# One-hot tables of the first expert layer: three wide vector operations a group in place of seventeen

## The reference

```python
eidx = jnp.take_along_axis(cidx, sel, axis=-1)
g = jax.nn.softmax(best, axis=-1)
act = jax.nn.gelu(jnp.einsum('td,thkd->thk', xb, u[eidx]).astype(jnp.float32))
return jnp.einsum('thk,thkd->td', (g * act).astype(v.dtype), v[eidx]).astype(h.dtype)
```

## Time and profile before

| | |
|---|---|
| median of 3 executions | 3064.28 us (3061.97 to 3066.18) |
| profiled execution | 3058.98 us, span 3057.2 us |
| the table, first DVE operation of a group to the last copy to `stage` | 799.24 to 893.86 us of the span |
| the stream's first multiply by gates | 923.97 us |
| DVE busy over the span | 2123.6 us, 69% |
| PE busy over the span | 2457.7 us, 80% |

### The profile page before, as it was taken

The page is one execution under the profiler, slowest core; times in us unless marked ns, Lnnn a source line. Parts: engine busy times, 40 slices in busy tenths (PEclk is TensorE's granted clock), DMA queues, the critical chain, the costliest instruction groups (busy, mean ns, idle before and its releaser), DMA issues. The chain is left out here.

```text
span 3057.2 us, 37030 instructions
## 1 busy us (share of the span) xinstructions
PE 2457.7 (80%) x13126; PEld 1869.5 (61%) x13126; DVE 2123.6 (69%) x4614; ACT 1117.4 (37%) x2622; POOL 881.5 (29%) x756
## 2 busy tenths in 40 slices
PE   5978798899469788888888888688787997777776
PEld 3778664576458687778777788478655642222222
DVE  3566662379968888888888798766644898745444
ACT  3432344334753333333333333342343443333332
POOL 1015100331003333434334343203203454333331
PEclk8985699899789889999989998797797999999998
DMA  5210105147269999999999999321002999999995
GB/s 213 81 32 1 51 14 206 57 145 269 97 263 363 414 414 412 414 412 414 409 414 413 409 407 414 113 80 32 9 17 103 403 421 421 422 421 422 422 421 240
DMA packets 175017, 816.63 MB, mean 267 GB/s; under 512 B 18584, under 2 KB 37592, under 8 KB 108400
## 3 DMA queue, kind: packets, MB, share of 16 engines
q0 software_dynamic: 73728, 536.90, 42.5%
q1 hardware_dynamic: 101104, 277.35, 24.2%
HBM read 796.37 MB, written 17.83 MB: 266 GB/s over the span
## 5 line engine op out<-in xcount | busy, mean ns | idle before, releaser
L2288 PE MATMUL ps<-peer_h,peer_u 128*128 128x256 f32 x2048 | 507.7, 405 | 161.4 <-DMA peer_u<-in_uT 161.3
L2262 POOL DMA_INDIRECT pair_ring<-in_uv_first,eid x256 | 390.5, 1525 | 797.1 <-DVE pair_sum L2412 286.4
L1945 PE MATMUL ps<-pair_ring,pair_diag 128*128 128x512 f32 x1024 | 475.2, 609 | 142.7 <-ACT pair_diag L2019 142.7
L2288 PEld LDWEIGHTS ps<-peer_h,peer_u 128*128 128x128 f32 x2048 | 409.7, 205 | 226.8 <-DMA peer_u<-in_uT 155.9
L2129 DVE CUSTOM_DVE_ANT_0 pair_ring<-pair_ring,hT 128x1024 f32<-128x1024 f32 x256 | 313.2, 1224 | 211.9 <-DMA pair_ring<-in_uv_rows,eid 211.9
L1945 PEld LDWEIGHTS ps<-pair_ring,pair_diag 128*128 128x128 f32 x1024 | 186.7, 192 | 420.4 <-ACT pair_diag L2019 231.1
L1909 POOL DMA_INDIRECT pair_ring<-in_uv_rows,eid x256 | 263.9, 1031 | 392.9 <-PE ps L1945 366.1
L119 PE MATMUL ps<-h_both 128*128 128x256 f32 x1024 | 313.4, 306 | 4.3 <-DVE h_both L2451 4.3
L2400 DVE CUSTOM_DVE_ANT_0 pair_ring<-pair_ring,hT 128x1024 f32<-128x1024 f32 x256 | 312.0, 1219 | 0.0
L121 PE MATMUL ps<-h_both 128*128 128x256 f32 x1024 | 289.8, 283 | 0.0
L120 PE MATMUL ps<-h_both 128*128 128x256 f32 x1024 | 289.8, 283 | 0.0
(11 more groups left out here) (406 smaller groups left out, 4686.3 us busy)
## 6 DMA issues: line engine op xcount, KB each, us to landing
peer_u<-in_uT SPq DMA_DIRECT2D x128, 512.0 KB, 24.5
peer_v<-in_uv_first SPq DMA_DIRECT2D x128, 512.0 KB, 22.5
ada_slab<-in_ada_w SPq DMA_DIRECT2D x20, 2048.0 KB, 8.3
proj_slab<-in_w_fm SPq DMA_DIRECT2D x38, 512.0 KB, 3.5
route_slab<-in_w_pq SPq DMA_DIRECT2D x32, 512.0 KB, 5.8
peer_gates<-dense_stage SPq DMA_DIRECT2D x4, 4096.0 KB, 13.1
peer_gates<-peer_gates SPq DMA_DIRECT2D x32, 512.0 KB, 27.4
out_slab<-in_w_out SPq DMA_DIRECT2D x16, 512.0 KB, 3.7
```

The costliest lines, as they stand in the source:

```text
L1945: mm = nc.tensor.matmul(ps[:, 4 + 2 * t + half, :], diag[:, s % DG, :], ring[:, s % R, D_MODEL + half * BANK:D_MODEL + (half + 1) * BANK], ...
L2262: nc.gpsimd.indirect_dma_start(out=ring[:, s % R], out_offset=None, in_=d["uv_first"], in_offset=bass.IndirectOffsetOnAxis(ap=eid[:, s // ...
L2288: mm = nc.tensor.matmul(ps[:, e % 2, 0:n], us[:, e % SW, k, :], hw[:, k, :], start=(k == 0), stop=(k == DC - 1))
```

## The change

1. `hot_i` is made in two operations. `same`, a new two-byte tile (bf16) with two buffers, takes one comparison of 16x128 values: `iT16`, a bf16 copy of `iT`, each value repeated 128 times along the innermost dimension, against `iota16`, a bf16 copy of `iota`, repeated over the 16 tokens. One product of 16x128 values, `same` by `gT` (fp32, each value repeated 128 times), then writes `hot_i`. The two copies are made once, with a wait for both.
2. DVE's order in a group becomes: comparison for i, comparison for j, product. `same_done` is a new semaphore between the first and the last.
3. `UJ` goes from 10 to 11: DVE writes 11 columns of `hot_j`, ACT 5.
4. The hardware loops become unrolled Python loops on all engines, and the columns for the group that does not exist, with the spare columns of `njT`, go.
5. The tiles are laid out anew. `iT16` and `iota16` take 192 words at the start, and what stands behind them in the stream moves up by 192 words (`hot_i` and `hot_j` too); `stage` keeps its place. `same` lies where ring slot 2 lies. `FREE` goes from 3 to 2, and the gather at `FREE` waits for the last `a_done` (the last `hot_i`) as well as for `stored[0]`.

```diff
             UJ = 10 -> 11
-            FREE = 3
+            FREE = 2
...
+                sb(st, f"dense_own{l}", [P, 192])
                 hot_i = sb(st, f"hot_i{l}", [P, 2, U, NKEY])
                 hot_j = sb(st, f"hot_j{l}", [P, 2, U, NKEY])
-                njT = sb(st, f"dense_nj{l}", [P, n + U])
-                sb(st, f"dense_gap{l}", [P, 10192])
+                njT = sb(st, f"dense_nj{l}", [P, n])
+                sb(st, f"dense_gap{l}", [P, 7936])
+                same = sb(st, f"dense_same{l}", [P, 2, U, NKEY], BF16)
+                sb(st, f"dense_end{l}", [P, 32])
                 stage = sb(st, f"dense_stage{l}", [P, 2, NKEY, TB])
...
                             if s == FREE:
-                                pool.wait_ge(stored[0], 16 * (n // (U * UB)))
+                                pool.wait_ge(a_done, GROUPS)
+                                pool.wait_ge(stored[0], 16 * (ntb // 2))
...
-                                if not (first and q < 2):
-                                    dve.wait_ge(g_mm, u - 1)
-                                nc.vector.tensor_tensor(hot_j[:, r, 0:UJ], bc(jT[:, bass.ds(u * U, UJ)], 2, NKEY),
-                                                        bc(iota[:], 1, UJ), ALU.is_equal).then_inc(b_done, 1)
-                                for t in range(U):
-                                    at = bass.ds(u * U + t, 1)
-                                    last = nc.vector.tensor_scalar(hot_i[:, r, t], iota[:], iT[:, at], gT[:, at],
-                                                                   ALU.is_equal, ALU.mult)
-                                last.then_inc(a_done, 1)
+                            if u >= 2:
+                                dve.wait_ge(a_done, u - 1)
+                            nc.vector.tensor_tensor(same[:, r], bc(iT16[:, u * U:(u + 1) * U], 2, NKEY),
+                                                    bc(iota16[:], 1, U), ALU.is_equal).then_inc(same_done, 1)
+                            if u >= 2:
+                                dve.wait_ge(g_mm, u - 1)
+                            nc.vector.tensor_tensor(hot_j[:, r, 0:UJ], bc(jT[:, u * U:u * U + UJ], 2, NKEY),
+                                                    bc(iota[:], 1, UJ), ALU.is_equal).then_inc(b_done, 1)
+                            dve.wait_ge(same_done, u + 1)
+                            nc.vector.tensor_tensor(hot_i[:, r], same[:, r], bc(gT[:, u * U:(u + 1) * U], 2, NKEY),
+                                                    ALU.mult).then_inc(a_done, 1)
```

More of the change, by code:

```diff
@@ L2174, in phase_experts @@
             SW = 4
-            FREE = 3
+            FREE = 2
             BACK = NS // 2 + LAG + 4
             steps = NKEY + LAG
-            a_done, b_done, g_mm, g_ev, neg_done, dist_done, c_done = (
-                sem(f"dense_{x}{l}") for x in ("a", "b", "mm", "ev", "neg", "dist", "c"))
+            a_done, b_done, g_mm, g_ev, neg_done, dist_done, c_done, same_done = (
+                sem(f"dense_{x}{l}") for x in ("a", "b", "mm", "ev", "neg", "dist", "c", "same"))
             stored = [sem(f"dense_stored{l}_{r}") for r in range(2)]
@@ L2235, in load_gates @@
                             sp.dma_start(gs[:, b % 2].rearrange("p b i t -> p b (i t)"), src).then_inc(g_in[b % 2], 16)
[L2237 to L2241, removed]
+                        for b in range(ntb):
+                            sp.wait_ge(g_ev, PB * (b + 1))
+                            sp.dma_start(gates_dram[b], stage[:, b % 2]).then_inc(stored[b % 2], 16)
                         sp.wait_ge(g_mm, GROUPS)
@@ L2246, in _ @@
                         for r in range(2):
[L2247 removed]
+                            sp.wait_ge(stored[r], 16 * (ntb // 2))
                         load_gates(0)
@@ L2267, in _, with table @@
                     def _(pe):
[L2268 to L2274, removed]
-                                if not (first and q < 2):
-                                    pe.wait_ge(g_ev, u - 1)
-                                for t in range(U):
-                                    mm = nc.tensor.matmul(ps[:, 4 * r + t // 4, (t % 4) * P:(t % 4 + 1) * P],
-                                                          hot_j[:, r, t], hot_i[:, r, t], start=True, stop=True)
-                                mm.then_inc(g_mm, 1)
+                        def table(u):
+                            r = u % 2
+                            pe.wait_ge(b_done, u + 1)
+                            pe.wait_ge(a_done, u + 1)
+                            pe.wait_ge(c_done, u + 1)
+                            if u >= 2:
+                                pe.wait_ge(g_ev, u - 1)
+                            for t in range(U):
+                                mm = nc.tensor.matmul(ps[:, 4 * r + t // 4, (t % 4) * P:(t % 4 + 1) * P],
+                                                      hot_j[:, r, t], hot_i[:, r, t], start=True, stop=True)
+                            mm.then_inc(g_mm, 1)
                         def hidden(e):
@@ L2306, in turn_back @@
                             mm.then_inc(tr_mm, 1)
-                        table(0, True)
-                        with pe.Fori(1, n // (U * UB)) as it:
-                            table(it, False)
+                        for u in range(GROUPS):
+                            table(u)
                         pe.wait_ge(g_ev, GROUPS)
@@ L2329, in columns @@
                             for t in range(UJ, U):
-                                last = nc.scalar.activation(hot_j[:, r, t], iota[:], ACT.Abs, bias=njT[:, bass.ds(u * U + t, 1)])
+                                o = u * U + t
+                                last = nc.scalar.activation(hot_j[:, r, t], iota[:], ACT.Abs, bias=njT[:, o:o + 1])
                             last.then_inc(dist_done, 1)
@@ L2334, in columns, with table @@
                                                  bias=onecol[:]).then_inc(c_done, 1)
[L2336 to L2339, removed]
+                        def table(u):
+                            if u + 1 < GROUPS:
+                                if u:
                                     act.wait_ge(g_mm, u)
[L2341 to L2347, removed]
+                                columns(u + 1, (u + 1) % 2)
+                            act.wait_ge(g_mm, u + 1)
+                            b, o = u // PB, (u % PB) * U
+                            if b >= 2 and o == 0:
+                                act.wait_ge(stored[b % 2], 16 * (b // 2))
+                            got = ps[:, 4 * (u % 2):4 * (u % 2) + 4, :].rearrange("p b (t i) -> p i (b t)", i=NKEY)
+                            nc.scalar.activation(stage[:, b % 2, :, o:o + U], got, ACT.Copy).then_inc(g_ev, 1)
                         def weight(s):
@@ L2355, in weight @@
                                                  scale=gate[:, s // NS, s % NS:s % NS + 1]).then_inc(swt_done, 1)
-                        act.wait_ge(neg_done, 2)
+                        act.wait_ge(neg_done, 1)
                         columns(0, 0)
-                        table(0, True)
-                        with act.Fori(1, n // (U * UB)) as it:
-                            table(it, False)
+                        for u in range(GROUPS):
+                            table(u)
                         for step in range(steps):
@@ L2419, in add_back @@
                             last.then_inc(back_done, 1)
-                        nc.vector.memset(njT[:, n:], 0.0).then_inc(neg_done, 1)
-                        nc.vector.tensor_scalar(njT[:, 0:n], jT[:], -1.0, None, ALU.mult).then_inc(neg_done, 1)
+                        nc.vector.tensor_scalar(njT[:], jT[:], -1.0, None, ALU.mult).then_inc(neg_done, 1)
                         nc.vector.memset(wt[:], 0.0).then_inc(zeroed, 1)
-                        table(0, True)
-                        with dve.Fori(1, n // (U * UB)) as it:
-                            table(it, False)
+                        dve_chain.mark(nc.vector.tensor_copy(iT16[:], iT[:]))
+                        dve_chain(dve, nc.vector.tensor_copy(iota16[:], iota[:]))
+                        for u in range(GROUPS):
+                            table(u)
                         nc.vector.tensor_tensor(hw[:], f32(hp[0][:]), f32(hp[1][:]), ALU.add).then_inc(h_whole, 1)
```

5 lines of the change are left out of this document (3 added, 2 removed).

## The result

The changed kernel takes 3074.85 us (median of 8, 3071.76 to 3083.13) against 3064.40 for the kernel before (8). The ratio is 1.0037, with a 95% interval of 1.0027 to 1.0048. Forecast were 3076.7 us and +12.4; measured +10.5 by the medians, +11.3 by the ratio. The profiled execution took 3074.86 us, with a span of 3073.1.

The account below looks back on a forecast made before the run. DVE was taken to bound the table and DMA transfers the stream after it. Table +7.0, gather gate +2.7 and one more gather +2.7 gave +12.4 us, median 3076.7 us; likeliest case 3070 to 3081, whole range 3059 to 3082.

Parts of the forecast that it names:

- The comparison: DVE's i comparison in a table group: taken at the slower rate, 2.296 us, for 2048 two-byte columns with a repeated value.
- the bounds: Two possible times for the i comparison: 1.226 us (two-byte, consecutive elements) or 2.296 us (fp32 of that length).
- the quick row: Profile row of a two-byte operation of 2048 columns, all operands through consecutive elements: 1.226 us, two columns a clock step.
- The sum of a group: DVE's table group: i comparison 2.21, j comparison 1.54, product 2.21, together 5.96 us against 5.50, 0.46 more.
- The table: All 16 groups of the table: end at 895.0 against 888.0, 7.0 us later.
- The gathers: Seam after the table: gather at FREE 9.7 us late (2.7 beyond the table), one more gather in the backlog 2.7 us.
- The end: First multiply by gates, and the stream and layers behind it: 12.4 us later, median 3076.7 us.
- the unrolling: Loops of the table written out on all engines: claimed to cost nothing.
- Hidden gathers: Rival at the seam: DMA slack hides the gathers, only the table's 7.0 us remain, 3071.3 us; chance 0.13.
- Quick and same: Rival in the table: quick comparison, group 4.89 us, the gather gate keeps the gain to -4.7 us, 3059.6; chance 0.10.
- Quick and faster: Rival: quick comparison and hidden gathers, all 10.0 us come through, 3054.3 us; chance 0.04.
- PE as the bound: Rival in the table: granted clock at 1.2 GHz makes PE pace groups, at most 3 us more, 3079.7; chance 0.03.

Follow-up runs that it names:

- row_repeat: Kernel after, the i comparison reading the first 128 values of iT16 as a row repeated per token (table not the reference's); ratio to before 0.9982.
- pairs: Kernel after with each i stored twice and the pair repeated one dimension out, FREE and gather wait as before the change; 3055.47 us against 3064.15, ratio 0.9969.
- gate_only: Kernel before with only FREE going from 3 to 2 and the gather at FREE also waiting for the last hot_i; ratio to before 1.0023.
- ten_columns: Kernel after with UJ back at 10; ratio to before 1.0020.
- gate_back: Kernel after with FREE at 3 again, no gather waiting for hot_i, and same lying where peer_h will lie; ratio to before 1.0027.
- turned_read: Kernel after with same laid out tokens innermost, the product reading it 16 elements apart, and the gathers as in gate_back; ratio to before 1.0040.
- pairs_ten: As pairs, with UJ = 10 (ten columns for DVE, six for ACT); ratio to before 0.9972.
- unroll_only: Kernel before with the hardware loops unrolled and the columns of the group that does not exist gone; ratio to before 0.9988.
- keys_outer: As turned_read, with hot_i also tokens innermost, so PE reads it 16 words apart; ratio to before 1.0056, and 1.0054 with UJ = 10.

## Why the prediction was right

**The comparison** was the step that decided, and it held: 2.281 us where I took 2.296. The choice between the bounds was argued, not shown, in the prediction; `row_repeat` and `pairs` show it, since only the steps of the comparison change and its time falls to 1.21 and 1.22. The reason that I gave for it was half right: I wrote that the quick row owes its rate to neighbours that differ, but in `pairs` the neighbours are equal and the rate is there. What counts in these runs is the step, not the values. The rule of the Trainium skill, "Vector Engine (DVE) Microarchitecture Reference", §5.1, agrees with the traces here (a repeated innermost element 2.28 us, a repeated row 1.21). The 1224 ns of the Trainium skill, "VectorE: DVE Perf Modes", section on the perf-mode tier table, is met only by the comparisons whose innermost step is 1 (1214 to 1231 ns).

**The sum of a group.** Forecast 2.21 + 1.54 + 2.21 = 5.96; measured 5.94, start to start 2.21, 1.53 and 2.21. The product from a bf16 and an fp32 operand ran at the fp32 rate, 2.281.

**The table.** Forecast 7.0 us later, measured 6.7 at the last `hot_i` and 6.7 at the last copy (102.1 against 95.4).

**The gathers.** Forecast 9.7 us for the gate, measured 9.6. Forecast 2.7 for one more gather; from the gate to the first multiply it is 42.5 us against 38.6, so 3.9. The difference has two parts.

- The first gather's instruction takes 2.74 us after this gate and 0.95 before, and the engines move nothing before it has ended (39 GB/s on average from 893 to 897). These 1.8 us the prediction put at nothing. In the twelve traces 52 gathers stand between the gate and the first multiply. 33 take 0.93 to 0.98 us; the other 19 each end 0.78 to 0.82 us behind the end of a two-tensor operation of DVE that was running when they started or came right behind one that was. The wait for the last `hot_i` puts the first gather behind such an operation every time: the sum that DVE writes to `peer_h` next, at 892.68 after. DVE's sixteen small operations held up no gather (0.95 and 0.98 before, at 885.41 and 886.67). This is read off the traces; no run moved `peer_h`.
- From the end of that instruction to the first multiply it is 39.7 us against 37.6, so 2.1 for the gather of 1.05 MB. The other kernels say 2.4: 38.6 us in `gate_only`, `row_repeat` and `ten_columns`, with gather 2 behind the gate, and 36.1 to 36.5 in `gate_back`, `turned_read`, `pairs`, `pairs_ten` and `unroll_only`, without it. (The two `keys_outer` kernels, with 39.3, are left out: their gate opens 14.5 us or more before the last copy of the table, in place of 5.5 to 11.3.) So the term is right and a little large.

That `gate_only` has only 2.8 us more than before from the gate to the first multiply, so near to the 2.7, is in part luck: the 1.8 us of the late start are in it as well, and its engines moved 398 GB/s in the backlog against 387 before.

**The end.** 13.5 us at the first multiply, forecast 12.4, in one profiled execution. The medians say 10.5 and the ratio 11.3 with an interval of 8.3 to 14.7, so the two agree within what can be measured. So the 12.4 is right to about a microsecond, with a missing 1.8 and an extra gather priced 0.3 to 0.6 too high beside each other. A part may also be the unrolling, which I put at nothing and which measured -0.1% by a bare margin.

**The rivals.** Hidden gathers: excluded by `gate_only`. Quick and same: it is `row_repeat`, 3059.6 forecast relative to 3064.3, -4.7 against a measured -0.18%, which is -5.5 (-8.9 to -2.5). Quick and faster: not with this gather; it needs the gather's part undone, as in `pairs`. **PE as the bound** was the weakest place: I said that a lower clock would cost at most 3 us by pacing every group. The clock did fall, but in single groups and without pacing the table after the change, as the last section tells.

## What to carry to other kernels

The two-byte comparison of two tensors had its double rate (1.21 to 1.23 us for 2048 columns) in every kernel here in which the innermost step of all its operands is 1, and lost it (2.28) where one operand repeats a value innermost. Such a value can be stored twice and repeated as a pair, which leaves all other access in order (1.22). Before a tile is put where a prefetch used to land, price the prefetch: here the slot and its wait cost 5.9 us, and the rest of the change 7.6. And if a stage ends in a full transfer queue, count when the first byte of that queue may leave, and how many bytes it holds, not only when the stage's compute ends. And look at what DVE does when POOL is to issue the first gather: behind a two-tensor operation it took up to 4.58 us here (`turned_read`) in place of 0.94.

## What was not expected of the hardware

The granted clock fell inside the table. Before, it was 1.00 throughout from 811 to 888, with PE idle 1.69 us in each group of 5.50. After, PE is idle 2.13 us in a group of 5.94, and the clock dips. Timeline of PE in the kernel after, and its granted clock by stretches:

```profile
851.29 5.44 PE L2279 MATMUL ps<-hot_i,hot_j 128*128 128x128 f32 x32 [2.13 <-issue]
857.23 3.81 PE L2279 MATMUL ps<-hot_i,hot_j 128*128 128x128 f32 x32 [0.50 <-issue]
...
875.04 5.44 PE L2279 MATMUL ps<-hot_i,hot_j 128*128 128x128 f32 x32 [2.13 <-issue]
```

```profile
853.00:859.00 6.00, 5.50 (x42) 5.34 (x41) 6.00 (x4) 2.62 (x4) 0.00 (x0) 0.85 1.02 437
859.00:865.00 6.00, 3.87 (x35) 3.71 (x34) 6.00 (x4) 5.82 (x12) 0.00 (x0) 1.00 0.42 178
...
875.00:881.00 6.00, 5.46 (x33) 5.33 (x33) 6.00 (x4) 2.59 (x7) 0.00 (x0) 0.72 1.02 437
```

Behind the start of the table, the fifth, ninth and thirteenth group run partly at 1.2 GHz (the granted clock is 0.50 from 852 to 854 and 1.00 from 855 on) and take 5.4 us in place of 3.81; the ones between run at the full 2.4 GHz. DVE's 5.94 us cover this, except where something waits for that very group: in `gate_back` it was the twelfth, behind which the third store and the gate stand, and the last, which moved the end of the table by 1.6 us (last copy at 103.7, after 102.1). In `ten_columns`, where PE waits 2.00 us a group, four groups take 5.44; in `pairs` and `row_repeat`, where it waits 1.06, none does and the clock is 1.00 throughout from 811 to 875. No run changed PE's wait alone, so why a given group is hit stays open.

How a gather's instruction is held up by DVE, as told under "The gathers", was not expected either: the prediction took the distance from the gate to the first bytes as it was before.

PE's price for reading the moving operand with a step of 16 words was new too: 6.97 us for 16 fp32 products against 3.81.
